# Rotary embedding by half-tile copies and element-wise sums instead of a rotation matmul, in a fused two-block transformer kernel

## The reference, cut to what matters

```python
def apply_rope(x, cos, sin):
    half = x.shape[-1] // 2
    x1, x2 = x[..., :half], x[..., half:]
    return jnp.concatenate([x1 * c - x2 * s, x2 * c + x1 * s], axis=-1)

q = apply_rope(q.reshape(B, S, 2 * H, d), cos, sin)     # d = 64, differential attention
k = apply_rope(k.reshape(B, S, 2 * H, d), cos, sin)
k_rope = apply_rope(k_rope, cos, sin)                   # latent attention, one shared key
q_rope = apply_rope(q[..., MLA_NOPE:], cos, sin)
```

## Time and profile before

| | |
|---|---|
| time, three executions | 1211.36 us median (1207.56, 1211.36, 1212.23) |
| profiled execution, its own time | 1207.88 us |
| its span from first to last instruction | 1206.6 us |
| busy: PE, DVE, ACT, POOL | 1148.1, 803.9, 620.7, 53.0 us |
| mean granted PE clock | 0.988 of full speed |
| first stage, `roped` from 621.2 to 704.0 us | 16 of the 21 rotary tiles |
| second stage, from 937.7 to about 1004.5 us | 5 of the 21 |

### The profile page before, as it was taken

How to read it: one execution, slowest core, us unless ns; L and a number is a source line. 1 busy time by engine, 2 the same in 40 slices (tenths; PEclk the granted TensorE clock), 3 DMA queues, 4 the chain that set the end, 5 groups by cost and what they waited for, 6 DMA issues and landing times.

```text
span 1206.6 us, 19169 instructions
## 1 busy us (share of the span) xinstructions
PE 1148.1 (95%) x7554; PEld 1050.4 (87%) x7554; DVE 803.9 (67%) x1332; ACT 620.7 (51%) x1138; POOL 53.0 (4%) x71
## 2 busy tenths in 40 slices
PE   4999999899999999999999899999998889999997
PEld 4988899699988899999889789999997778999996
DVE  4878888787756756565758867655557665655655
ACT  5645444646655544444645445555457344645543
POOL 3100000000000000000012110000000100000000
PEclk8999999999999999999999999999999999999999
DMA  8969998373322565654342334555554413655530
GB/s 339 408 255 415 350 344 319 140 283 137 105 85 91 196 242 212 215 205 175 140 175 106 106 105 164 186 185 199 175 193 146 151 36 125 241 175 194 191 140 36
DMA packets 34009, 231.75 MB, mean 192 GB/s; under 512 B 3704, under 2 KB 5120, under 8 KB 6528
## 3 DMA queue, kind: packets, MB, share of 16 engines
q1 hardware_dynamic: 31952, 226.24, 51.3%
q10 hardware_dynamic: 1968, 4.29, 1.1%
HBM read 229.45 MB, written 1.06 MB: 191 GB/s over the span
## 4 chain that ended last, share of the span: by engine, by line
PE 78%; DVE 11%; ACT 7%; issue 2%; DMA 1%; POOL 1%; DVEq 0%; SPq 0%; ACTq 0%; POOLq 0%
PE ps L396 36%; PE pacc L396 34%; DVE wlo L359 3%; ACT whi L358 2%; PE ps L406 2%; PE ps L409 2%; ACT wk L1194 2%; PE pacc L406 1%; DVE st L1189 1%; ACT arena L675 1%; POOL st L525 1%; DMA raw<-in_stream 1%; DMA cst<-in_const 1%; PE pacc L409 1%; DVE raw L336 0%
## 5 line engine op out<-in xcount | busy, mean ns | idle before, releaser
L359 DVE TENSOR_TENSOR wlo<-raw,whi 128x1024 fp32r<-128x1024 f32 x353 | 429.8, 1226 | 173.8 <-ACT whi L358 166.4
L358 ACT ACTIVATE whi<-raw 128x1024 fp32r<-128x1024 f32 x353 | 368.3, 1055 | 151.6 <-PE pacc L396 72.3
L396 PE MATMUL ps<-nhi,whi 128*128 128x256 f32 x1256 | 363.3, 289 | 2.4 <-DVE arena L1473 1.0
L396 PE MATMUL ps<-nlo,whi 128*128 128x256 f32 x1256 | 357.5, 285 | 0.0
L396 PE MATMUL ps<-nhi,wlo 128*128 128x256 f32 x1256 | 357.4, 285 | 0.0
L396 PEld LDWEIGHTS ps<-nhi,whi 128*128 128x128 f32 x1256 | 242.8, 193 | 8.4 <-DVE arena L1473 1.3
L396 PEld LDWEIGHTS ps<-nlo,whi 128*128 128x128 f32 x1256 | 242.8, 193 | 4.3 <-issue 0.5
L396 PEld LDWEIGHTS ps<-nhi,wlo 128*128 128x128 f32 x1256 | 242.8, 193 | 0.0
L915 ACT ACTIVATE sg<-ps 128x256 f32<-128x256 f32 x104 | 39.8, 383 | 159.6 <-PE ps L396 159.6
L396 PE MATMUL pacc<-whi,mhi 128*128 128x512 f32 x240 | 95.5, 398 | 0.0
L396 PE MATMUL pacc<-wlo,mhi 128*128 128x512 f32 x240 | 94.1, 392 | 0.0
(11 more groups left out here) (333 smaller groups left out, 1775.2 us busy)
## 6 DMA issues: line engine op xcount, KB each, us to landing
raw<-in_stream SPq DMA_DIRECT2D x213, 1024.0 KB, 4.9
gates<-in_g_post ACTq DMA_DIRECT2D x3, 512.0 KB, 8.2
h<-in_x SPq DMA_DIRECT2D x1, 1024.0 KB, 7.1
cst<-in_const ACTq DMA_DIRECT2D x1, 1024.0 KB, 4.7
arena<-bias_rows ACTq DMA_DIRECT2D x1, 1024.0 KB, 14.5
out<-tmp SPq DMA_DIRECT2D x4, 256.0 KB, 2.2
silu_c<-in_c_row ACTq DMA_DIRECT2D x1, 512.0 KB, 5.9
arena<-in_final_g SPq DMA_DIRECT2D x1, 512.0 KB, 3.6
```

The lines of the kernel that those rows point to most:

```text
L358: t_hi = act.do(lambda e: e.activation(whi[:, s, :], src, ACT.Copy), arrived, room)
L359: t_lo = dve.do(lambda e: e.tensor_tensor(wlo[:, s, :], src, whi[:, s, :].bitcast(F32), ALU.subtract), arrived, room, t_hi)
L396: return e.matmul(o, lt[a], rh[b], start=start and first, stop=stop and last)
```

## The change

The weight columns of every rotary block are reordered on the host (`halves_first`), so that the first halves (32 columns) of both 64-wide groups stand on partitions 0 to 63 and the second halves on 64 to 127. The exchange of halves is then a copy of 64 partitions to the other 64. ACT makes it: two copies of 64x256 out of PSUM into a new buffer `turned`, beside the full copy it made before. The sign moves into the sine table. The rotation matmul and its constant are gone, and the block's bank is given back after ACT's copies. One place later DVE multiplies by the sines and adds once. For a query tile a third part follows one more place later: ACT writes both tiles, each as a full 128x256 copy whose per-partition scale is a column `own` of ones and zeros. With the new order, the two 64-wide groups are told apart by bit 5 of the partition number, so `own` has ones in alternate groups of 32.

`rope_end` no longer stays in the list of active parts after its work is done. In the second stage the query's rotary tile is ready one block later than before (after block `2g+1` instead of `2g`). The keys' tiles are marked ready at the same place as before.

```diff
+        own = mod[:, 33:35]
+        t_zero = pool.do(lambda e: e.memset(own, 0.0), t_half)
+        for q in range(4):
+            t_zero = pool.do(lambda e: e.memset(own[32 * q:32 * q + 32, q % 2:q % 2 + 1], 1.0), t_zero)
+        t_own = t_zero
...
+        turned = sb("turned", [P, 2, T])
+        rs_ = Rooms([Room(turned[:, n, :]) for n in range(2)])
 
         def roped(o, b, tk, s, cos=cos, sin=sin, t_tables=None):
 
-            xb, yb = xs.take(), ys.take()
+            xb, yb, xr = xs.take(), ys.take(), rs_.take()
             t = act.do(lambda e: e.activation(xb.ap, b.ap[:, 0:T], ACT.Copy, scale=s), tk, xb.free)
+            for to, of in (lohi, lohi[::-1]):
+                t1 = act.do(lambda e: e.activation(xr.ap[to, :], b.ap[of, 0:T], ACT.Copy, scale=s), tk, xr.free)
+            banks.give(b, t1)
             t0 = pool.do(lambda e: e.tensor_tensor(yb.ap, xb.ap, cos, ALU.mult), t, yb.free, t_tables)
             yield
-            tk = put_last(b.ap[:, T:2 * T], rotm, xb.ap, True, t)
-            turned = o if o.shape[1] == T else xb.ap
-            t = dve.do(lambda e: e.tensor_tensor(turned, b.ap[:, T:2 * T], sin, ALU.mult), tk,
-                       [] if turned is o else t0, t_tables)
-            banks.give(b, t)
-            if turned is o:
-                t = [dve.do(lambda e: e.tensor_tensor(o, o, yb.ap, ALU.add), t, t0)]
-            else:
-                t = [dve.do(lambda e: e.tensor_tensor(o[q, c, :], xb.ap[q, :], yb.ap[q, :], ALU.add), t, t0)
-                     for c, q in enumerate(lohi)]
-            xs.give(xb, *t)
-            ys.give(yb, *t)
-            yield t
+            t1 = dve.do(lambda e: e.tensor_tensor(xr.ap, xr.ap, sin, ALU.mult), t1, t_tables)
+            key = o.shape[1] == T
+            t = dve.do(lambda e: e.tensor_tensor(o if key else xb.ap, xr.ap, yb.ap, ALU.add), t0, t1)
+            ys.give(yb, t)
+            rs_.give(xr, t)
+            if not key:
+                yield
+                t = [act.do(lambda e: e.activation(o[:, c, :], xb.ap, ACT.Copy, scale=own[:, c:c + 1]), t, t_own)
+                     for c in range(2)]
+            xs.give(xb, *(t if not key else [t]))
+            yield t if not key else [t]
...
         def rope_end(at, rope):
-            t_q[at], born[at] = next(rope), side.now
-            yield
+            t = next(rope)
+            if t is None:
+                yield 1
+                t = next(rope)
+            t_q[at], born[at] = t, side.now
...
-                if pend is not None:
-                    t_qr[pend[0]], born[pend[0]] = next(pend[1]), side.now
-                    pend = None
+                t = next(pend[1])
+                if t is not None:
+                    t_qr[pend[0]], born[pend[0]] = t, side.now
...
+def halves_first(w):
+
+    k, m = w.shape
+    return w.reshape(k, m // P, 2, 2, 32).transpose(0, 1, 3, 2, 4).reshape(k, m)
```

More of the change, by code:

```diff
@@ L45 @@
 _at = 0
-for _name, _n in (("ident", 128), ("ones", 128), ("rot", 128), ("tri", 128), ("causal", 128), ("strict", 128), ("flip", 128),
+for _name, _n in (("ident", 128), ("ones", 128), ("tri", 128), ("causal", 128), ("strict", 128), ("flip", 128),
                   ("cos", 256), ("sin", 256), ("topk", 512), ("bucket", 384)):
@@ L516, in build @@
         lohi = (slice(0, 64), slice(64, 128))
-        t_zero = t_half
+        own = mod[:, 33:35]
[3 more added lines that the diff above has]
+        t_own = t_zero
         for c in range(2):
@@ L1439, in build @@
         t_g8 = dve.do(lambda e: e.tensor_scalar(g8, col("subln_g"), 1.0 - LAMBDA0, None, ALU.mult))
-        cos, sin, rotm = const_of("cos"), const_of("sin"), const_of("rot")
+        cos, sin = const_of("cos"), const_of("sin")
         def scaled_tables(cross, at):
@@ L1761, in constants @@
     put("ident", np.eye(P))
[L1762 to L1768, removed]
     put("flip", np.eye(P)[::-1])
@@ L1776, in constants @@
     put("cos", np.cos(ang).astype(np.float32).T[i % 32])
-    put("sin", np.sin(ang).astype(np.float32).T[i % 32])
+    put("sin", np.where(i[:, None] < 64, -1.0, 1.0) * np.sin(ang).astype(np.float32).T[i % 32])
     t = np.arange(T)
@@ L1816, in lay_out @@
     w = v["w_qkv_a_2"][0]
-    src["qk"] = tiles_T(w[:, 0:2048])
+    src["qk"] = tiles_T(halves_first(w[:, 0:2048]))
     src["v"] = w[:, 2048:3072].reshape(8, P, D)
@@ L1821, in lay_out @@
     src["dkv"] = w[:, 0:256].reshape(2, 4, P, 256).transpose(0, 2, 1, 3).reshape(2, P, 1024)
-    src["dkr"] = tiles_T(np.concatenate([w[:, 256:320], w[:, 256:320]], axis=1))
+    src["dkr"] = tiles_T(halves_first(np.concatenate([w[:, 256:320], w[:, 256:320]], axis=1)))
     w = v["w_ukv_2"].reshape(256, 8, 256)
@@ L1828, in lay_out @@
     w = v["w_uq_2"][0].reshape(384, 8, 192)
-    w = np.concatenate([w[:, :, 0:128].reshape(384, 1024), w[:, :, 128:192].reshape(384, 512)], axis=1)
+    w = np.concatenate([w[:, :, 0:128].reshape(384, 1024), halves_first(w[:, :, 128:192].reshape(384, 512))], axis=1)
     w = tiles_T(w)[UQ_ORDER].transpose(1, 0, 2).reshape(P, 36 * P)
```

## The result

The changed kernel takes 1213.41 us (median of 15; 1209.68 to 1215.86) against 1209.62 us (median of 15; 1206.89 to 1212.23) for the kernel before. The ratio is 1.0029 with a 95% interval of 1.0017 to 1.0041: a loss of some 3.5 us, inside the half per cent that counts as no change, where 1204 was forecast. The forecast's gain was 7.3 us, taken from a median of 1211.36 us of three executions; over all fifteen that kernel's median is 1.7 us lower.

The account below looks back on a forecast made before the run. PE was taken to bound the kernel, except mid first stage, where a DVE, ACT and POOL loop sets the pace. Gains of 5.3 (first stage) and 2.0 us (second) sum to 7.3, from median 1211.36 to 1204 us; 8-in-10 range 1197 to 1211.

Parts of the forecast that it names:

- 22 us on ACT. It has cover: Both stages: added ACT copies total 22 us; a first-stage turn's 1.9 us fits in 4.27 us of ACT idle time.
- The split runs four blocks ahead: First stage: the weight split queued on ACT behind the tile copies runs four blocks ahead; no cost counted for it.
- if the cover is gone, each turn pays up to 1.9 us: First-stage turns: should ACT's idle time not cover the added copies, each turn would lose up to 1.9 us.
- ACT's tile copies ending a wait of PE: Sign in the profile after that the prediction is wrong: ACT's tile copies end PE's waits, meaning cover gone.
- PE's waits for the rotary copy: First-stage turns: PE waits 0.9 us per turn for ACT's copy before the rotation matmul; no such wait expected after.
- the first rival: PE bounds it all: 9.0 us of rotations and the waits behind them come off, 16 us, giving 1195.4; chance 0.12.
- The bank wait: First stage's end: PE's PSUM bank wait moves one head on, about 5 us at L1555, ended by exponentials.
- 5.3 (3 to 8): First stage: gain of 5.3 us, bounds 3 (clock falls fully) and 8 (no fall, shorter wait).
- the softmax waits: Second stage: PE waits 1.6 to 2.4 us for the second head's softmax in each of three turns.
- I take 2.0, near the upper end: Second stage: gain between 0.1 and 2.5 us, taken as 2.0 because two other waits go too.
- the clock rival: Both stages: clock falls in each of nine turns or waits, costing 15.3 us, giving 1218.2; chance 0.09.
- the gain stops at the loops: Both stages: softmax waits fully replace PE waits and first stage gains only 3, total 2.6 us, giving 1208.8; chance 0.28.

Follow-up runs that it names:

- e4: Kernel before plus two spare ACT copies of 64x256 per rotary tile that nobody reads; ratio 1.0043 to the kernel before.
- e15: e14 plus two spare ACT copies of 64x256 per rotary tile; ratio 1.0023 to the kernel before.
- e8: Changed kernel with the weight split issued ahead of the rotary copies in the first stage; ratio 0.9993 to the kernel before, first stage 108.48 us.
- e10: e8 with the second stage's rotation back on PE, in e5's order there; ratio 0.9968 to the kernel before, second stage 79.64 us.
- e11: e8 with each second-stage head's transposes issued half a block later; 1200.97 us, ratio 0.9929 to the kernel before.
- e14: e5 with each second-stage head's transposes issued half a block later, rotation still on PE; ratio 0.9979 to the kernel before.
- e13: Changed kernel with only each second-stage head's transposes issued half a block later; ratio 0.9979 to the kernel before, second stage 76.64 us.
- e5: Kernel before with only the change's new times at which heads start, rotation still on PE; ratio 0.9997 to the kernel before.
- e12: e9 plus two spare ACT copies of 64x256 per rotary tile; ratio 1.0067 to the kernel before.
- e9: e5 (rotation on PE) with the weight split issued ahead of the rotary copy in the first stage; ratio 1.0047 to the kernel before.

## Why the prediction was wrong

The step that failed is "22 us on ACT. It has cover". It set ACT's idle time in one turn of the kernel before (4.27 us) against the added time per turn (1.9), as if every turn after the change were that turn, and did not ask what stands behind the added copies. With the heads' new order the turns are no longer alike. In every second one ACT has three split copies and six half copies, the idle time before the exponentials is down to 1.09 us, and the added copies stand on the chain ahead of the split's copy. "The split runs four blocks ahead" is true of PE's need for the weights. It is not true of DVE, which issues its own half (L359) in order and stops for ACT's: 2.0 us in each long turn. The prediction's own sentence, "if the cover is gone, each turn pays up to 1.9 us", was the case to weigh: two of four turns paid 2.2 over the forecast (12.6 against 10.4) and the other two nothing, 1.1 on average. One of its signs of being wrong, ACT's tile copies ending a wait of PE, is there too, once and with 1.0 us. That ACT's load has a price is shown by e4 (5.2 us without any gain), that the turns pay it only in the new order by e4 against e15, and how much hangs on the split's place by e8 (4.4 us, with the clock that came back in it).

A smaller part is the duration. The copies of one half onto the other came 0.40 us apart (0.78 for two; 0.86 for e4's two), not 0.28, and ACT's busy time rose by 28.1 us, not 22. On DVE a multiplication or sum sometimes took 0.83 to 0.96 us instead of 0.42 (0.49 on average), which is part of why it lost 3.3 us and not 5; what doubles them was not looked into.

What held: PE's waits for the rotary copy are gone. (There were two of 0.9 us in the DVE-bound turns, not one in each, as the text and the first rival's 3 x 0.9 have it; the forecast does not hang on it.) The bank wait moved to head 6; it is 3.4 us at its scores (L406) rather than 5 at L1555, and the multiplication of a result ends it, not exponentials. In e8, head 6's exponentials start at 693.66 us where 693.0 was forecast, and the first stage gains 3.6 us (2.8 and 5.1 in e10 and e11) where 5.3 (3 to 8) was forecast. That lies within the bounds, but in part by luck: head 5's exponentials start at 684.74, where 682.6 was forecast, and head 6's only 8.9 us later instead of 10.4, while the mean turn is 10.71 and not 10.4.

In the second stage the softmax waits were sized rightly: 1.6 to 2.4 us in each of three turns, measured 6.6 in 3, the longest 2.3. What failed is the balance "I take 2.0, near the upper end": two other waits remained (1.0 and 0.8), and the clock fell, which I had weighed only as a rival for all turns. Five rotations less, with 3.1 us more of idle time, gave PE the same busy time at 0.92 of full clock: +3.1 us instead of -2.0. So the clock rival holds in part: a fall at about 966 us and one from 991 to 1001, and in the first stage half clock inside the long turns (0.90 and 0.87 over the two turns, where the turns before had 1.00 but for the last). It is nothing like its 15 us. The Trainium skill ("TensorE: Matmul & The Clock Gate", "HAM oscillation — how this bites in real kernels") has loops that wait in every turn start each turn at half clock; here it held in some turns and not in others. The rival "the gain stops at the loops" named a smaller gain, not a loss.

The exchange itself is worth about what was forecast (7.3 us) once it is scheduled for what it is: e11 is 6.0 us faster than e14, which has the same second stage order and PE's rotation (0.9979 to 0.9929), each with the split where it is better. With the split behind, e13 and e14 are equal: what it takes off PE it costs on ACT.

Open is what made the clock fall in the changed kernel's long turns and not in e8's, and in its second stage and not in e5's, where PE idles about as long in one stretch (below); the longest single waits differ (2.3 us in the changed kernel's second stage and 1.5 in e5's; in the four turns 2.6 us in the changed kernel and 2.2 in e8). e12's load costs 5.7 us in the second stage in its profile and 2.4 over the whole kernel by the medians: 4.2 of the 5.7 are PE's busy time, at a clock of 0.92 against 0.98, and e9's profile lies 3.2 us below its median.

## What to carry to other kernels

Idle time of an in-order engine covers added work only as long as no other engine waits for what now stands behind it: in e4 the spare copies ran into the idle time and the turns stayed as they were, in the changed kernel DVE stopped for the split behind them. So read the timeline from the added work on, name what stands behind it and who needs that, and count turn by turn: a change of order can put the work of three tiles into one turn and leave the mean looking harmless. When a producer's consumer changes (a matmul at once, or an element-wise operation a place later), the best place of what is issued beside it can change too: the same swap of two calls was worth -4.4 us with the exchange and +6 without. Test an edit together with the two or three places that it frees, and with the same places on the kernel before as a control.

## What the runs showed of the hardware

In these traces the granted clock does not follow from the idle share of a stretch. In e5, stretches of 5 us:

```profile
981.96:986.96 5.00, 2.46 (x16) 1.68 (x15) 3.83 (x10) 3.12 (x8) 0.83 (x1) 1.00 0.01 2
986.96:991.96 5.00, 5.00 (x32) 4.54 (x31) 2.54 (x5) 1.88 (x4) 0.00 (x0) 1.00 0.11 16
```

PE was busy for 2.46 of 5 us at full clock and had full clock behind it, while the changed kernel, busy for 4.17 of 5, was granted 0.63 and then 0.69 while PE was full.

ACT's groups by shape, after: a copy of 64x256 to the other half of the partitions, a plain copy of 128x256 out of PSUM, and one with a scale column (count, busy us, mean ns, idle before).

```profile
L1487 ACT ACTIVATE arena<-sg,mod 128x256 f32<-128x256 f32 x24 | 10.8, 498 | 2.1 <-DVE sg L1482 2.1
L1476 ACT ACTIVATE turned<-ps 64x256 f32<-64x256 f32 x28 | 10.6, 379 | 0.7
L1474 ACT ACTIVATE sg<-ps 128x256 f32<-128x256 f32 x14 | 5.4, 386 | 4.0 <-PE ps L396 3.9
```

Half the partitions cost as much as all of them (379 against 386 ns), so the exchange by two half copies pays two full copies.
